# Expert down products with 64-column weight halves as the stationary operand, results transposed one expert later

## The reference, cut to what matters

```python
aff = softmax(h @ w_router)                    # tokens x 16
gate, idx = top_k(aff of each expert, cap)     # cap 64 (sample), 16 (prompt)
xs = h[idx]                                    # 80 slots x 1024 for each expert
hid = silu(xs @ w_gate[e]) * (xs @ w_up[e])    # 80 x 1024
out = (hid @ w_down[e]) * gate                 # 80 x 1024
x = x + g2 * scatter_add(out at idx)
```

## Time and profile before

| | us |
|---|---|
| median of 3 runs | 3237.7 (3235.4 to 3247.43) |
| the profiled execution, whole | 3238.82 |
| its span | 3237.0 |
| TensorE busy in the span | 2777.5 (86%) |
| VectorE, ScalarE, GpSimd busy | 759.1, 572.8, 187.9 |
| moved by DMA | 514.10 MB, mean 159 GB/s |

### The profile page before, as it was taken

How to read it: one execution, slowest core, us unless ns; L and a number is a source line. 1 busy time by engine, 2 the same in 40 slices (tenths; PEclk the granted TensorE clock), 3 DMA queues, 4 the chain that set the end, 5 groups by cost and what they waited for, 6 DMA issues and landing times.

```text
span 3237.0 us, 77145 instructions
## 1 busy us (share of the span) xinstructions
PE 2777.5 (86%) x34814; PEld 1908.1 (59%) x34814; DVE 759.1 (23%) x1313; ACT 572.8 (18%) x1109; POOL 187.9 (6%) x200
## 2 busy tenths in 40 slices
PE   4679778599999895999999987995648799999998
PEld 3445446489888653667676644553624466767664
DVE  0033055555554513000000011004752200000001
ACT  1110235433333202100000001004321110000000
POOL 1000000233322100000000000000000000000000
PEclk8689868699999896999999998997979799999999
DMA  9921000000000120499999821101001059999981
GB/s 375 337 73 52 7 2 0 14 4 3 4 4 4 65 78 1 183 381 390 400 392 398 329 69 42 52 29 51 0 13 78 1 210 377 399 394 395 395 308 46
DMA packets 161373, 514.10 MB, mean 159 GB/s; under 512 B 14116, under 2 KB 17856, under 8 KB 161088
## 3 DMA queue, kind: packets, MB, share of 16 engines
q1 hardware_dynamic: 151216, 489.45, 39.6%
q10 hardware_dynamic: 8608, 18.33, 2.1%
q0 software_dynamic: 1392, 3.87, 0.4%
HBM read 497.06 MB, written 6.16 MB: 155 GB/s over the span
## 4 chain that ended last, share of the span: by engine, by line
PE 68%; issue 7%; DVE 6%; DMA 4%; PEld 4%; DVEq 2%; ACT 2%; ACTq 1%; POOLq 0%; POOL 0%; PEldq 0%; SPq 0%
PE ps L1546 14%; PE ps L1559 14%; PE ps L455 8%; PE ps L1006 7%; PE ps L1654 4%; PE ps L1506 4%; DMA big<-w_exp_down 3%; PEld ps L457 2%; PE ps L457 2%; PE ps L1014 2%; PE ps L1091 2%; PEld ps L455 1%; PE ps L707 1%; PE ps L716 1%; PE ps L432 1%
## 5 line engine op out<-in xcount | busy, mean ns | idle before, releaser
L455 PE MATMUL ps<-hT,ring 128*128 128x512 f32 x912 | 474.9, 603 | 73.8 <-DVEq L507 33.5
L1546 PE MATMUL ps<-rs,ring 128*64 128x80 f32 x12288 | 442.3, 233 | 6.5 <-issue 6.3
L1546 PEld LDWEIGHTS ps<-rs,ring 128*64 128x64 f32 x12288 | 430.1, 137 | 24.9 <-issue 23.9
L457 PEld LDWEIGHTS ps<-hT,ring 128*128 128x128 f32 x912 | 175.2, 192 | 221.9 <-issue 221.9
L1624 DVE TENSOR_TENSOR big<-big,ps 128x320 f32<-128x320 f32 x64 | 28.3, 484 | 998.0 <-PE ps L1559 964.2
L1559 PE MATMUL ps<-big 128*80 128x512 f32 x512 | 226.9, 596 | 0.9
L1559 PE MATMUL ps<-ring,big 128*80 128x512 f32 x512 | 225.0, 592 | 2.4 <-DVE big L1624 2.4
L1006 PE MATMUL ps<-big 64*64 64x64 f32 x5440 | 204.7, 226 | 5.9 <-issue 5.9
L455 PEld LDWEIGHTS ps<-hT,ring 128*128 128x128 f32 x912 | 140.4, 194 | 76.6 <-issue 40.6
L1006 PEld LDWEIGHTS ps<-big 64*64 64x64 f32 x5440 | 180.0, 139 | 9.1 <-issue 6.6
L457 PE MATMUL ps<-hT,ring 128*128 128x128 f32 x912 | 176.7, 276 | 0.0
(11 more groups left out here) (379 smaller groups left out, 3144.2 us busy)
## 6 DMA issues: line engine op xcount, KB each, us to landing
ring<-w_exp_up SPq DMA_DIRECT2D x124, 1024.0 KB, 9.6
ring<-w_exp_gate SPq DMA_DIRECT2D x68, 1024.0 KB, 10.7
big<-w_exp_down SPq DMA_DIRECT2D x64, 1024.0 KB, 10.5
ring<-w_exp_down SPq DMA_DIRECT2D x64, 1024.0 KB, 10.8
big<-w_exp_gate SPq DMA_DIRECT2D x60, 1024.0 KB, 9.8
ring<-w_ada SPq DMA_DIRECT2D x12, 2048.0 KB, 18.3
big<-w_ada SPq DMA_DIRECT2D x12, 2048.0 KB, 18.5
ring<-w_in_odd SPq DMA_DIRECT2D x6, 2048.0 KB, 8.8
```

Source lines behind the costliest of these rows:

```text
L455: nc.tensor.matmul(ps[2 * pair][:, :], blocks[s][:, k, j * P:(j + 1) * P], rhs(k, 0, TS), start=(k == 0), stop=(k == KC - 1))
L457: last = nc.tensor.matmul(ps[2 * pair + 1][:, 0:TP], blocks[s][:, k, j * P:(j + 1) * P], rhs(k, TS, T), start=(k == 0), stop=(k == KC - 1))
L1546: last = nc.tensor.matmul(ps[2 * m + j // 4][a:a + HALF, (j % 4) * SLOTS:(j % 4 + 1) * SLOTS], ex_blocks[ex_slot(q)][:, k % 2, j * P + a:j ...
```

## The change

Three things change in the expert loop, and one outside it.

- `down` uses the form of gate_up: two opening matmuls, then for each block 32 matmuls with a weight half as the stationary operand and 80 slots of `hid` streaming. The result stands in banks 4 and 5 with features on the partitions.
- ScalarE copies it to a new buffer `outT` (`evict`). One expert later, between gate and up, TensorE transposes it with 8 transposes into banks 6 and 7 (`turn`), and ScalarE copies from there to `oute` and issues the two DMAs as before (`out`). Two semaphores are added, `evicted` and `turned`.
- The first loop turn is written out ahead of the loop, `gate_up(1, 0)` and `down(1, 8)`, and after the last down stand `turn(E)` and `turn(E + 1)`.
- Elsewhere semaphores are merged (three that told of a square root taken become one that counts, and so on). The instructions there stay as they are.

```diff
@@ -1364,6 +1364,7 @@
         zeros = fr(2 * SLOTS)
         blank = zeros.bitcast(mybir.dt.bfloat16)
         oute = fr(D)[0:SLOTS, :]
+        outT = fr.three(KC, SLOTS)
         slots = rs[:, :].rearrange("p (k s) -> p k s", k=KC)
         wrt = fr.three(KC, E)
         slotT, aff = (fr.three(NT, E) for _ in range(2))
@@ -1530,41 +1531,61 @@
             def loaded(x, at):
                 pe.wait_ge(arrived[ex_slot(at)], ex_fills(l, x, at))
 
-            def gate_up(x, at):
+            def opened(b):
+                for f in range(2):
+                    nc.tensor.matmul(ps[b + f][:, 0:4 * SLOTS], blank[:, 0:P], blank, start=True, stop=False)
+
+            def products(b, q, k, rhs):
+
+                for j in range(8):
+                    for a in (0, HALF):
+                        last = nc.tensor.matmul(ps[b + j // 4][a:a + HALF, (j % 4) * SLOTS:(j % 4 + 1) * SLOTS],
+                                                ex_blocks[ex_slot(q)][:, k % 2, j * P + a:j * P + a + HALF],
+                                                rhs[:, k, :], start=False, stop=(k == KC - 1 and j % 4 == 3))
+                return last
+
+            def gate_up(x, at, between=None):
                 pe.wait_ge(sem(u + "staged"), x + (l * (E + 1) + 2))
                 for m in range(2):
                     if at == 0:
                         pe.wait_ge(sem(u + ("hidden" if m else "silu")), x * 2 + 2 * l * E)
-                    for f in range(2):
-                        nc.tensor.matmul(ps[2 * m + f][:, 0:4 * SLOTS], blank[:, 0:P], blank, start=True, stop=False)
+                    opened(2 * m)
                     for b in range(4):
                         q = at + 4 * m + b
                         loaded(x, q)
                         for k in range(2 * b, 2 * b + 2):
-                            for j in range(8):
-                                for a in (0, HALF):
-                                    last = nc.tensor.matmul(ps[2 * m + j // 4][a:a + HALF, (j % 4) * SLOTS:(j % 4 + 1) * SLOTS],
-                                                            ex_blocks[ex_slot(q)][:, k % 2, j * P + a:j * P + a + HALF],
-                                                            slots[:, k, :], start=False, stop=(k == KC - 1 and j % 4 == 3))
+                            last = products(2 * m, q, k, slots)
                         last.then_inc(used, 1)
+                    if m == 0 and between:
+                        between()
 
             def down(x, at):
                 pe.wait_ge(sem(u + "hidden"), x * 2 + 2 * l * E)
-                pe.wait_ge(sem(u + "out_kept"), x + l * (E + 1))
+                pe.wait_ge(sem(u + "evicted"), x + l * (E + 1))
+                opened(4)
                 for b in range(4):
                     q = at + b
                     loaded(x, q)
                     for k in range(2 * b, 2 * b + 2):
-                        for f in range(2):
-                            last = nc.tensor.matmul(ps[4 + f][0:SLOTS, :], hid[:, k, :], ex_blocks[ex_slot(q)][:, k % 2, f * W:(f + 1) * W],
-                                                    start=(k == 0), stop=(k == KC - 1))
+                        last = products(4, q, k, hid)
                     last.then_inc(used, 1)
 
+            def turn(x):
+                pe.wait_ge(sem(u + "evicted"), x + l * (E + 1))
+                pe.wait_ge(sem(u + "out_kept"), x + l * (E + 1) - 1)
+                for j in range(KC):
+                    last = nc.tensor.transpose(ps[6 + j // 4][0:SLOTS, (j % 4) * P:(j % 4 + 1) * P], outT[:, j, :], ident)
+                last.then_inc(sem(u + "turned"), 1)
+
             gate_up(0, 4)
-            with pe.Fori(1, E) as x:
-                gate_up(x, 0)
+            gate_up(1, 0)
+            down(1, 8)
+            with pe.Fori(2, E) as x:
+                gate_up(x, 0, lambda: turn(x))
                 down(x, 8)
             down(E, 0)
+            turn(E)
+            turn(E + 1)
 
         def experts_pool(pool, l):
             u = "ex_"
@@ -1590,28 +1611,38 @@
                 for f in range(2):
                     nc.scalar.activation(gs[f], ps[f][:, 0:4 * SLOTS].rearrange("p (k s) -> p k s", k=4), ACT.Silu)                        .then_inc(sem(u + "silu"), 1)
 
-            def out(n, p, x, at):
+            def evict(x, at):
+                act.wait_ge(used, ex_done(l, x, at + 3))
+                act.wait_ge(sem(u + "turned"), x + l * E - 1)
+                for f in range(2):
+                    last = nc.scalar.copy(outT[:, 4 * f:4 * f + 4, :], ps[4 + f][:, 0:4 * SLOTS].rearrange("p (k s) -> p k s", k=4))
+                last.then_inc(sem(u + "evicted"), 1)
+
+            def out(n, p):
                 e = 2 * n + p
-                act.wait_ge(used, ex_done(l, x, at + 3))
+                act.wait_ge(sem(u + "turned"), e + (l * E + 1))
                 act.wait_ge(sem(u + "out_moved"), e * 32 + 32 * (l * (E + 1) + 1))
                 for f in range(2):
-                    last = nc.scalar.copy(oute[:, f * W:(f + 1) * W], ps[4 + f][0:SLOTS, :])
+                    last = nc.scalar.copy(oute[:, f * W:(f + 1) * W], ps[6 + f][0:SLOTS, :])
                 last.then_inc(sem(u + "out_kept"), 1)
                 act.wait_ge(sem(u + "out_kept"), e + (l * (E + 1) + 2))
                 act.dma_start(outS[CAP_S * p:CAP_S * (p + 1), ds(n, 1), :], oute[0:CAP_S, :].unsqueeze(1)).then_inc(sem(u + "out_moved"), 16)
                 act.dma_start(prompt_rows[l, ds(e * CAP_P, CAP_P), :], oute[CAP_S:SLOTS, :]).then_inc(sem(u + "out_moved"), 16)
 
             act.drain().then_inc(sem(u + "out_kept"), 1)
+            act.drain().then_inc(sem(u + "evicted"), 1)
             act.drain().then_inc(sem(u + "out_moved"), 32)
             silu(0, 4)
-            with act.Fori(0, E // 2 - 1) as n:
-                silu(2 * n + 1, 0)
-                out(n, 0, 2 * n + 1, 8)
-                silu(2 * n + 2, 0)
-                out(n, 1, 2 * n + 2, 8)
-            silu(E - 1, 0)
-            out(E // 2 - 1, 0, E - 1, 8)
-            out(E // 2 - 1, 1, E, 0)
+            silu(1, 0)
+            evict(1, 8)
+            with act.Fori(1, E // 2) as n:
+                for p in range(2):
+                    silu(2 * n + p, 0)
+                    out(n - 1, p)
+                    evict(2 * n + p, 8)
+            evict(E, 0)
+            out(E // 2 - 1, 0)
+            out(E // 2 - 1, 1)
             act.wait_ge(sem(u + "out_moved"), 32 * (E + 1) * (l + 1))
 
         def experts_dve(dve, l):
...
@@ -576,8 +576,8 @@
             for c in range(9):
                 nc.scalar.activation(kscr[:, c, :], kk[:, c, :] if c < 4 else proj[:, Q0 + c - 4, :], ACT.Square)\
                     .then_inc(sem("head_squared"), 1)
-            act.wait_ge(sem("head_mean"), 1)
-            nc.scalar.activation(head_rows, head_rows, ACT.Sqrt).then_inc(sem("head_root"), 1)
+            act.wait_ge(sem("head_rows"), 1)
+            nc.scalar.activation(head_rows, head_rows, ACT.Sqrt).then_inc(sem("roots_taken"), 1)
 
         def headnorm_pe(pe):
...
```

More of the change, by code:

```diff
@@ L588, in headnorm_pe @@
                 last = nc.tensor.matmul(ps[1][0:18, 0:TP], to_rows[:, c, :], kscr[:, c, TS:T], start=(c == 0), stop=(c == 8))
-            last.then_inc(sem("head_summed"), 1)
-            pe.wait_ge(sem("head_inverse"), 1)
+            last.then_inc(sem("heads_summed"), 1)
+            pe.wait_ge(sem("head_rows"), 2)
             for c in range(9):
@@ L599, in headnorm_dve @@
         def headnorm_dve(dve):
-            dve.wait_ge(sem("head_summed"), 1)
+            dve.wait_ge(sem("heads_summed"), 1)
             for src, a, b in ((ps[0][0:18, :], 0, TS), (ps[1][0:18, 0:TP], TS, T)):
@@ L604, in headnorm_dve @@
             nc.vector.tensor_scalar(head_rows, head_rows, row_norm[:, 2:3], None, ALU.add)
-            dve.drain().then_inc(sem("head_mean"), 1)
-            dve.wait_ge(sem("head_root"), 1)
+            dve.drain().then_inc(sem("head_rows"), 1)
+            dve.wait_ge(sem("roots_taken"), 1)
             nc.vector.reciprocal(head_rows, head_rows)
-            dve.drain().then_inc(sem("head_inverse"), 1)
+            dve.drain().then_inc(sem("head_rows"), 1)
             for c in range(9):
@@ L1276, in rwkv_end_pe @@
                 last = nc.tensor.matmul(ps[7][0:H, 0:TP], end_to[:, c, 0:H], scr[:, c, TS:T], start=(c == 0), stop=(c == RC - 1))
-            last.then_inc(sem("rend_summed"), 1)
+            last.then_inc(sem("heads_summed"), 1)
             pe.wait_ge(sem("rend_rows"), 2)
@@ L1294, in rwkv_end_act @@
             act.wait_ge(sem("rend_rows"), 1)
-            nc.scalar.activation(end_rows, end_rows, ACT.Sqrt).then_inc(sem("rend_root"), 1)
+            nc.scalar.activation(end_rows, end_rows, ACT.Sqrt).then_inc(sem("roots_taken"), 1)
             for c in range(RC):
@@ L1313, in rwkv_end_dve @@
                 last.then_inc(empty, 1)
-            dve.wait_ge(sem("rend_summed"), 1)
+            dve.wait_ge(sem("heads_summed"), 2)
```

(6 more changed lines are left out.)

## The result

The changed kernel takes 3312.4 us (median of 4 runs, 3300.7 to 3322.0); the kernel before, run again beside it, 3239.4 us (3235.4 to 3247.4). The ratio is 1.022, with a 95% interval of 1.0175 to 1.0266: slower, by some 73 us; whether by more than 2% the interval leaves open. The profiled execution of the changed kernel took 3320.4 us, so its stages are set against the 3238.8 us of the profiled execution before: +81.6 us.

What follows compares the result with a forecast made beforehand. It took the expert turns to stand on TensorE and transfers 0.1 us apart, with transfers setting them afterwards. Layer sums of +0.7 and +5.1 us, rounded up to +7 on 3237.7, gave 3245 us, range 3230 to 3365.

Steps and rivals of the forecast that it cites:

- rival 1: Expert loop: the longer body is refetched every turn, +113 us a layer, mildest +30; chance 0.38 layer 1 alone, 0.17 both.
- layer 1 alone: Case in which only layer 1's expert loop body is fetched again: 3275 to 3358 us, chance 0.38.
- TensorE's work in a turn: Steady expert turn: three products of 28.2 us in all plus eight transposes of 1.04 make 29.2, saving 3.3 us.
- The transfers' pace: Steady expert turn: unchanged bytes set it at 32.7 to 33.0 us; +1.5 us in layer 0, +0.2 in layer 1.
- Rival 2: Expert loop: loads released sooner move faster, a turn of 32.0 us saves 22 us, giving 3223; chance 0.07.
- The end of the stage: End of each expert stage: TensorE follows the last load by 2.25 us, gaining 9.6 us in layer 0, 9.2 in layer 1.
- When the loads are done: Last expert load of each layer: later by 6 us for code, plus 1.5 us of pace in layer 0, 0.2 in layer 1.
- Instruction packets: Expert stages: 9.7 more packets of code per layer delay the loads by 6 us a layer, between 0.5 and 9.3.
- the body stays: Case in which neither layer's loop body is refetched: +0.7 and +5.1 us, 3245 us, own range 3231 to 3261, chance 0.38.
- The tail: Last down to scatter, two outputs in succession: 16.3 us in layer 1 (+7.0, +1.1 low clock), 20.8 in layer 0 (+2.8).

Runs made afterwards that it cites:

- half_up: l1_pad16 with half of each up block left unread within the loop, so its output is not the reference's: 3142.7 us, one run.
- before_late_out: The kernel before with ScalarE's two output DMAs issued after the next silu, in mid-turn: 3241.1 us, one run, beside 3236.2.
- l1_pad16: The changed kernel with 16 nearly idle instructions (8 small matmuls) ahead of layer 1's experts: 3222.7 us beside 3236.2 for the kernel before, ratio 0.9954.
- before_peeled: The kernel before with only its first expert loop turn written out ahead of the loop: 3244.0 us, one run, beside 3236.2.
- l0_pad104: The changed kernel with 104 nearly idle instructions ahead of layer 0's experts: 3225.0 us, one run.
- l0_pad110: The changed kernel with 55 small matmuls (110 instructions) ahead of layer 0's experts: 3300.5 us, one run.
- l0_pad142: The changed kernel with 71 small matmuls (142 instructions) ahead of layer 0's experts: 3331.0 us, one run.

## Why the prediction was right or wrong, by its steps

It forecast 3245 us with a range to 3365; the time is 3312.4, which is not its likeliest case but rival 1 in layer 1 alone, 3275 to 3358.

**TensorE's work in a turn.** Predicted 29.2, measured 29.04 in half_up. Right.

**The transfers' pace.** Predicted 32.67 to 33.0 us a turn, measured 32.11 in both layers once layer 1 fits. The step that failed is the reading of the landing times: that they grow by 0.12 us a turn does show that the transfers needed more than 32.55, but it was taken for what these bytes need however they are placed. It was the need of that order of things, with the write where it was. The rows of late layer 1, where the queue was full and the turn 33.02, were read as a ceiling for the same reason. Rival 2 (a turn of 32.0, given 0.07) had the right pace and named the right stretch, "the slower stretch in which the output is written". It expected a deeper queue to fill it; before_late_out shows that the moment of the write has a share, and what share the queue has is open.
Twelve loads of 1.049 MB and 0.33 MB written are 12.9 MB a turn, 402 GB/s in 32.11 us. The Trainium skill, "Perfetto Trace Analysis" (Roofline), puts the 16 DMA engines of a core together at about 435 GB/s, by which 12.9 MB would take 29.7 us, an estimate; no turn here came to that, but it would have spoken against reading 395 GB/s as the end of what they give.

**The end of the stage.** Predicted gains of 9.6 and 9.2 us from the last down ending closer behind the last load. By the DMA records of l1_pad16 the last load lands at 1846.7 and 3125.2 and the last down ends at 1850.6 and 3128.6, 3.9 and 3.4 us behind (3.6 in layer 0 of the changed kernel), not 2.25. It doesn't wait for that load: it starts once the down before it has ended and VectorE has written `hid` (1.2 us), and then runs its 9.4 to 9.7 us through. In the kernel before, the last load landed at 1848.7 and 3140.2; the prediction's 1849.4 took in the write of an output. So the gain is 8.7 and 8.4 us. The mechanism was right, and the size nearly.

**When the loads are done.** With code and pace in it, the prediction has the last load land 7.5 and 6.2 us later after the start of the stage than before. In l1_pad16 it lands 2.4 and 9.0 us earlier, 25 us off in all, where the case was 22 us too high. The larger part is the pace: thirteen turns at 32.11 instead of the 32.55 and 32.76 of before are -5.7 and -8.5, where +1.5 and +0.2 had been taken.

**Instruction packets.** Taken at 6 us a layer between bounds of 0.5 and 9.3. What the pace leaves of the 2.4 and 9.0 is +3.3 and -0.5 us for ten packets more a layer, 1.4 in the mean, near the lower bound; it is a difference of single executions, and before_peeled can't sharpen it. The step that failed is the choice of row: the slow rates of the first turns were put down to the packets that share the engines with the loads. What else slows the first turns wasn't tried. Of the 22 us by which the case "the body stays" was too high, about 9 are this term and 16 the pace; the end of the stage takes 2 back.

**The tail.** Predicted from the last down to scatter 16.3 us in layer 1 and 20.8 in layer 0. The chain of the changed kernel, layer 0 and then layer 1:

```profile
1850.71 1.01 PE ps L1577 x8
...
1854.09 6.72 DMA prompt_rows<-big
...
1862.52 5.48 DMA prompt_rows<-big
1868.03 4.97 DMA big<-prompt_rows
...
1873.05 9.69 PE ps L1685 x16
```

```profile
3226.67 1.01 PE ps L1577 x8
...
3230.06 2.69 DMA prompt_rows<-big
...
3234.46 2.69 DMA prompt_rows<-big
3237.17 4.88 DMA big<-prompt_rows
3242.10 9.54 PE ps L1685 x16
```

15.4 and 22.3: two landings in a row in both layers, as predicted. In layer 0 the second write took 5.48 us instead of the quiet 2.8; it had been taken to come after the crowd of the 2 MB loads, and didn't. The first scatter product takes 9.54 in layer 1 where it took 8.83: +0.7 of the +1.1.

**"The body stays": +0.7 and +5.1 us.** Measured in l1_pad16, whose body does stay: -6.6 and -11.2, in all 3222.7 us where the case had 3245 and its own range began at 3231.

**Rival 1.** The place was predicted: about 111 into a block in layer 0 and within five of a boundary in layer 1, measured 112 and one before. So was the risk that only layer 1 crosses. The form was not: every turn was to pay 8.7 us, +113 a layer. The chip pays in every second turn as a rule, 13.4 us over two turns of 32.1, or 6.7 a turn, and the stage is 98.9 us longer than in l1_pad16: six pairs at 13.4 are 80, the seventh stall and what follows it some 12, and 7 aren't accounted for. By the medians the price is 89.7 us (3312.4 - 3222.7), as the profiled execution of the changed kernel was 8 us above its median. Had the body stayed at the forecast's 3245 and one layer paid 90, the time would have been 3335; the 22 us by which that forecast was too high brought it down to 3312. The head of the loop costs more than the 5.8 taken for a back-edge (11.8, two blocks one after the other) and the later blocks less (2.9 once).
The Trainium skill, "Runtime: NRT & Kernel Launch" (Instruction fetch mechanics), gives TensorE's instruction memory 2048 instructions, eight blocks of 256. The runs agree with eight, in the form that the prediction gave it, seven and the one fetched ahead: seven stay down to the last instruction (l0_pad104), and six instructions in an eighth are too many (l0_pad110). The same section's statement of two lines is contradicted again, by a body of 1578 that stays.

**The choice between the cases.** "The body stays" and "layer 1 alone" had 0.38 each, and the first was taken because its price was one value. The body of layer 1 is six blocks and 42 instructions, so it touches seven when it begins at 214 or before, eight from 215 on. Within five of a boundary was even odds between the two, and that was the prediction's honest state; a count exact to one instruction, as the padded runs gave it, would have decided it. That the time fell in the stated range is in part luck: the range held both cases, and the case that was forecast is not the one that came.
Three sums of the prediction are slightly off, and nothing hangs on them: 6.2 x 5.8 + 5.8 is 41.8 and not 41.6, 29.2 + 5.8 is 35.0 and not 35.1, and the upper bound of the first case comes to some 3254 from its own terms, not 3256.

## What to carry to other kernels

A loop body long enough to near the capacity of the instruction memory has a place as well as a length: count its instructions, register steps too, for each copy of the loop by itself (here two layers of one source differ by two), find its start within a block of 256 from the stalls of the first pass, and shift it by a few idle instructions before anything else is concluded about the change; here 16 of them were worth 90 us, and turned a loss of 2% into a gain of 0.5%. In a trace, look for instruction packets in steady turns and for "issue" at the loop's head.

Landing times that grow from turn to turn show that transfers need more than the turn as things are ordered now. They don't show what they would need if small writes came at another moment.

## What the runs showed of the hardware

A loop body of TensorE of 1576 or 1578 instructions stays when it touches seven blocks of 256, down to the last instruction of the seventh (l0_pad104). With six instructions in an eighth it costs 71 us a stage of fourteen turns (l0_pad110), with 38 or 41 some 100 (l0_pad142, the changed kernel).

The blocks are fetched again in every second turn as a rule: nine packets in the stalled turn, and one turn of 29.0 us behind it without a stall. The stall at the head is mostly 11 to 12 us for two blocks under full transfers, and takes the granted clock down with it: 0.76 over the next product, 11.54 us instead of 9.01.

One core moved 402 GB/s over a whole turn of 1 MB loads, with landings at 14.1 us, where the order of before had 392 once its transfers set the turn.
